# Second expert table: 768 of its 2048 columns read whole and multiplied, the other 1280 gathered

## The reference, cut to what matters

```python
sc = einsum('thcd,hckd->thck', qry, sub_keys)            # 256 tokens, 8 heads, 2 halves, 128 keys
top_s, top_i = top_k(sc, 16)
cand_s = top_s[:, :, 0, :, None] + top_s[:, :, 1, None, :]
cand_i = top_i[:, :, 0, :, None] * 128 + top_i[:, :, 1, None, :]
best_s, best_pos = top_k(cand_s, 16)
idx, gates = take_along_axis(cand_i, best_pos), softmax(best_s)
u   = expert_down[ib]                                    # 128 rows of 2048 for each token
act = gelu(einsum('tkd,td->tk', u, xb))
vv  = expert_up[ib]                                      # 128 rows of 2048 for each token
out = einsum('tk,tkd->td', gates * act, vv)
```

## Time and profile before

| | |
|---|---|
| median of three runs | 2442.86 us |
| the profiled execution, its time | 2440.96 us |
| its span, first to last instruction | 2439.2 us |
| busy: TensorE matmuls, VectorE, ScalarE, GpSimd | 2017.3, 1354.1, 623.8, 630.3 us |
| moved by DMA over the span | 727.64 MB, mean 298 GB/s |
| of it by the gathers | 536.90 MB |
| expert stage: first gather, last added row | 539.0 us, 1882.5 us |

### The profile page before, as it was taken

One profiled execution on the slowest core, in us unless ns is written; L12 is line 12 of the kernel. 1 busy time (PEld: TensorE's weight loads), 2 busy tenths in 40 slices (PEclk: granted clock), 3 DMA queues, 4 the chain that ended last, 5 costly groups with the idle time before them and its releaser, 6 DMA issues. The chain is left out here.

```text
span 2439.2 us, 21677 instructions
## 1 busy us (share of the span) xinstructions
PE 2017.3 (83%) x8013; PEld 1331.2 (55%) x8013; DVE 1354.1 (56%) x1820; ACT 623.8 (26%) x901; POOL 630.3 (26%) x523
## 2 busy tenths in 40 slices
PE   6999867984988989777777888898771899999975
PEld 5888746873444444322233434443220888999874
DVE  4446537447554556455555654665547755555444
ACT  4334325321011111111111111011001554354333
POOL 0000000006543544445355434444533000000000
PEclk9999958996999999999999999999996899999988
DMA  5555501729999999999999999999998544465531
GB/s 197 197 195 190 199 1 47 264 85 382 421 422 422 422 421 422 423 421 419 421 422 420 416 422 421 416 420 423 421 422 343 180 160 158 146 205 186 188 122 70
DMA packets 102203, 727.64 MB, mean 298 GB/s; under 512 B 11840, under 2 KB 11968, under 8 KB 19808
## 3 DMA queue, kind: packets, MB, share of 16 engines
q0 software_dynamic: 73728, 536.90, 53.1%
q1 hardware_dynamic: 28384, 189.52, 22.0%
HBM read 722.18 MB, written 4.19 MB: 298 GB/s over the span
## 5 line engine op out<-in xcount | busy, mean ns | idle before, releaser
L1248 PE MATMUL bank<-ring,work 128*128 128x512 f32 x1920 | 894.0, 609 | 240.1 <-DMA ring<-in_peer_up_dram,work 238.7
L1492 DVE CUSTOM_DVE_ANT_0 ring<-ring,mix_t 128x2048 f32<-128x2048 f32 x256 | 584.2, 2291 | 526.7 <-DMA ring<-in_peer_down_dram,work 526.5
L1248 PEld LDWEIGHTS bank<-ring,work 128*128 128x128 f32 x1920 | 350.5, 192 | 716.5 <-issue 504.3
L449 DVE TENSOR_TENSOR ring_r<-ring,ring_r 128x2048 fp32r<-128x2048 f32 (+2 forms) x150 | 320.0, 2136 | 319.4 <-ACT ring_r L428 319.0
L1376 POOL DMA_INDIRECT ring<-in_peer_down_dram,work x256 | 316.6, 1237 | 440.1 <-DVE work L1449 238.2
L1385 POOL DMA_INDIRECT ring<-in_peer_up_dram,work x240 | 284.4, 1185 | 480.4 <-PE bank L1248 421.6
L482 PE MATMUL bank<-ring_r,mix_r 128*128 128x512 f32 (+1 forms) x1248 | 393.2, 386 | 0.0
L428 ACT ACTIVATE ring_r<-ring 128x2048 fp32r<-128x2048 f32 (+2 forms) x150 | 267.6, 1787 | 307.1 <-DMA ring<-in_w_out_dram 90.4
L482 PE MATMUL bank<-ring_r,act_r 128*128 128x512 f32 (+1 forms) x864 | 309.4, 388 | 12.6 <-DVE ring_r L449 12.6
L1316 ACT ACTIVATE work<-const,work 128x128 f32<-128x128 f32 x240 | 91.5, 399 | 734.3 <-PE bank L1248 733.1
L482 PEld LDWEIGHTS bank<-ring_r,mix_r 128*128 128x128 f32 x1248 | 233.6, 188 | 43.5
(11 more groups left out here) (354 smaller groups left out, 1336.3 us busy)
## 6 DMA issues: line engine op xcount, KB each, us to landing
ring<-in_w_out_dram SPq DMA_DIRECT2D x32, 1024.0 KB, 4.8
ring<-in_w_in_qk_dram SPq DMA_DIRECT2D x24, 1024.0 KB, 4.8
ring<-in_w_in_rest_dram SPq DMA_DIRECT2D x24, 1024.0 KB, 4.8
ring<-in_w_in_mo_dram SPq DMA_DIRECT2D x24, 768.0 KB, 4.4
h<-in_w_query_dram SPq DMA_DIRECT2D x8, 2048.0 KB, 10.4
ring<-in_w_in_ml_oz_dram SPq DMA_DIRECT2D x12, 1024.0 KB, 4.8
h<-in_xa_wkv_dram SPq DMA_DIRECT2D x4, 2048.0 KB, 16.8
ring<-in_w_in_lru_dram SPq DMA_DIRECT2D x8, 1024.0 KB, 4.9
```

The costliest lines, as they stand in the source:

```text
L449: dve.tensor_tensor(low(c), raw(c), plain(high(c)), ALU.subtract).then_inc(k.weights_low, 1)
L1248: m = pe.matmul(B[c][:, :], diag[:, j % DEPTH, :], up_row(j)[:, c * 512:(c + 1) * 512], start=first, stop=last)
L1492: dve.tensor_tensor_reduce(down_row(j), down_row(j), xn[:, t, :], 1.0, 0.0, ALU.mult, ALU.add, dots[:, p, j:j + 1]).then_inc(down_used, 1)
```

## The change

The second table is stored as two: columns 0 to 767 (`peer_up_dense`, laid out as 128 blocks, one for each first key, of 128 second keys by 768) and columns 768 to 2047 (`peer_up_rest`).

- Of the 256 second-table gathers all remain, with 1280 columns (640 KB) instead of 2048. Five a unit ("near", 75 in units 1 to 15, of the unit before) are issued among the first-table gathers and added by TensorE, three matmuls each. The other 181 ("far") are issued after the last first-table gather, through four slots, and added by VectorE.
- For the 768 columns a matrix of coefficients is made for each tile: for each token q a product of two one-hot matrices of [row, key], one of them scaled by the coefficient, gives [second key, first key]. Four tokens make a group of one bank, which ScalarE copies into `w_t[t]`, 64 KB a partition. Tile 0's one-hots are made by ScalarE in units 8 to 14 (`first_hots`: 8 Abs, 1 Relu, 4 Copy for a group of four tokens); tile 1's by VectorE after the last unit, two instructions for each token.
- TensorE then multiplies all 128 blocks: SyncE loads a block of 384 KB (`dense`, four slots), and for each there are four products of 384 columns. VectorE adds the four banks at the end.
- The first table's gathers, their four slots, the selection and its place are as before. The four slots of the second table are now of 1280 columns, the rest of the half is for blocks and one-hots. Coefficients and expert numbers of all units are kept. `coef` of a unit is made at row 1 of the next.
- The memory's load comes at the stage's start; its transposes stand in unit 6 and its keys and values in units 6 to 8. The unit loops are written out instead of hardware loops.

```diff
 
 
+DENSE = 768
+REST = D - DENSE
+NEAR = 5
...
+    up_rows = shaped(k.ring[:, 0:DEPTH * REST], DEPTH, REST)
+    dense_rows = shaped(k.ring[:, DEPTH * REST:8192], DEPTH, DENSE)
+    down_rows = shaped(k.ring[:, 8192:16384], DEPTH, D)
+    HOTS = 2 * DENSE // (2 * P)
+    hots = shaped(k.ring[:, 8192 - 2 * DENSE:8192 - 2 * DENSE + HOTS * 2 * P], HOTS, 2, P)
+    w_t = [shaped(k.first_weights[:, :], P, P), shaped(k.second_weights[:, :], P, P)]
+    cuts = [(at, min(512, REST - at)) for at in range(0, REST, 512)]
+    half = DENSE // 2
...
+    near = lambda n: [(NEAR * (n - 1) + i, i) for i in range(NEAR)] if n else []
+    NEAR_ALL = NEAR * (UNITS - 1)
+    far_of = [[(n, j) for n in range(t * PEER_H, (t + 1) * PEER_H) for j in range(NEAR if n < UNITS - 1 else 0, K)] for t in range(NT)]
+    shorter = min(map(len, far_of))
+    far = [of[i] for i in range(shorter) for of in far_of] + [r for of in far_of for r in of[shorter:]]
+    landed = lambda u: (up_in[u % DEPTH], 16 * (u // DEPTH + 1))
+
+    first_groups = [(n, j) for n in range(PEER_H, UNITS - 1) for j in BUILD_AT if n > PEER_H or j > 9][:GROUPS]
+    assert len(first_groups) == GROUPS
+    memory_parts = {(6 + (8 + i) // K, (8 + i) % K): (i // 8, (2 * i % 16, 2 * i % 16 + 1)) for i in range(32)}
...
+            def dense(i):
+                sp.dma_start(dense_rows[:, i % DEPTH, :], ins["peer_up_dense"][i]).then_inc(dense_in[i % DEPTH], 16)
+
+            sp.wait_ge(mem_turned, TURNS)
+            sp.wait_ge(coef_done, UNITS - 1)
+            dense(0)
+            dense(1)
+            sp.wait_ge(hot_used, 2 * P)
+            dense(2)
+            dense(3)
+            for i in range(DEPTH, P):
...
+            def add_row(u, i, n):
+                t = (n - 1) // PEER_H
+                first, last = (n - 1) % PEER_H == 0 and i == 0, n in (PEER_H, UNITS - 1) and i == NEAR - 1
+                if first and t:
+                    pe.wait_ge(acc_out, len(cuts))
+                pe.wait_ge(diag_ready, u + 1)
+                pe.wait_ge(*landed(u))
+                for b, (at, width) in enumerate(cuts):
+                    m = pe.matmul(B[b][:, 0:width], diag[:, u % 2, :], up_rows[:, u % DEPTH, at:at + width], start=first, stop=last)
+                m.then_inc(up_used, 1)
...
+            def build_group(t, g, depth):
+                n = t * GROUPS + g
+                if n == 0:
+                    pe.wait_ge(query_out, KV1)
+                if n >= 3:
+                    pe.wait_ge(weights_out, n - 2)
+                for e in range(4):
+                    q = 4 * g + e
+                    pe.wait_ge(hot_ready, t * P + q + 1)
+                    pe.matmul(bank_of(n)[:, e * P:(e + 1) * P], hots[:, q % depth, 0, :], hots[:, q % depth, 1, :],
+                                  start=True, stop=True).then_inc(hot_used, 1)
...
+            turn_indices(1)
+            for g in range(GROUPS):
+                build_group(1, g, HOTS)
+            pe.wait_ge(weights_out, 2 * GROUPS)
+            pe.wait_ge(acc_out, NT * len(cuts))
+            for i in range(P):
+                pe.wait_ge(dense_in[i % DEPTH], 16 * (i // DEPTH + 1))
+                for t in range(NT):
+                    for c in range(2):
+                        m = pe.matmul(B[2 * t + c][:, 0:half], w_t[t][:, i, :], dense_rows[:, i % DEPTH, c * half:(c + 1) * half],
+                                      start=i == 0, stop=i == P - 1)
+                m.then_inc(dense_used, 1)
...
+            def take_group(t, g):
+                n = t * GROUPS + g
+                act.wait_ge(hot_used, 4 * n + 4)
+                act.activation(w_t[t][:, :, 4 * g:4 * g + 4], shaped(bank_of(n)[:, :], 4, P).rearrange("p t i -> p i t"), ACT.Copy) \
+                   .then_inc(weights_out, 1)
+
+            def first_hots(g):
+
+                if g == 0:
+                    act.wait_ge(iota_in, 16)
+                    act.wait_ge(indices_out, 1)
+                    act.wait_ge(mem_turned, TURNS)
+                else:
+                    act.wait_ge(hot_used, 4 * g)
+                for e in range(4):
+                    q = 4 * g + e
+                    act.activation(hots[:, e, 0, :], iota, ACT.Abs, bias=turned[:, 1, q:q + 1], scale=-1.0)
+                    m = act.activation(hots[:, e, 1, :], iota, ACT.Abs, bias=turned[:, 0, q:q + 1], scale=-1.0)
+                step(m)
+                all4 = hots[:, 0:4, :, :].rearrange("p a b c -> p (a b c)")
+                step(act.activation(all4, all4, ACT.Relu, bias=k.c("ones")[:, 0:1], scale=-1.0))
+                for e in range(4):
+                    act.activation(hots[:, e, 0, :], hots[:, e, 0, :], ACT.Copy, scale=turned[:, 2, 4 * g + e:4 * g + e + 1]) \
+                       .then_inc(hot_ready, 1)
...
+            for n in range(UNITS):
+                rows_here = dict(zip(NEAR_AT, near(n)))
+                pool.wait_ge(selected, n + 1)
                 for j in range(K):
+                    d = n * K + j
+                    if d >= DEPTH:
+                        pool.wait_ge(down_used, d - DEPTH + 1)
+                    gather(down_rows[:, d % DEPTH, :], ins["peer_down"], rows[:, n, j:j + 1], down_in[d % DEPTH])
+                    if j in rows_here:
+                        u, i = rows_here[j]
+                        if u == 0:
+                            pool.wait_ge(mem_squared, NT)
+                        if u >= DEPTH:
+                            pool.wait_ge(up_used, u - DEPTH + 1)
+                        gather(up_rows[:, u % DEPTH, :], ins["peer_up_rest"], rows[:, n - 1, i:i + 1], up_in[u % DEPTH])
+            for f, (n, j) in enumerate(far):
+                u = NEAR_ALL + f
+                if f < DEPTH:
+                    pool.wait_ge(up_used, u - DEPTH + 1)
+                else:
+                    pool.wait_ge(far_used, f - DEPTH + 1)
+                gather(up_rows[:, u % DEPTH, :], ins["peer_up_rest"], rows[:, n, j:j + 1], up_in[u % DEPTH])
...
+            select(0, 0)
+            for n in range(UNITS):
+                p, t = n % 2, n // PEER_H
                 for j in range(K):
+                    if j == 1 and n:
+                        weigh(n - 1, 1 - p)
+                    if j == 2 and n == PEER_H + 1:
+                        take_sums(0)
+                    if j == DEPTH and n + 1 < UNITS:
+                        select(n + 1, 1 - p)
...
+                    d = n * K + j
+                    row = down_rows[:, d % DEPTH, :]
+                    dve.wait_ge(down_in[d % DEPTH], 16 * (d // DEPTH + 1))
+                    dve.tensor_tensor_reduce(row, row, xn[:, t, :], 1.0, 0.0, ALU.mult, ALU.add, dots[:, p, j:j + 1]) \
+                       .then_inc(down_used, 1)
+            take_sums(1)
+            weigh(UNITS - 1, 1)
+
+            dve.wait_ge(indices_out, 2)
+            dve.wait_ge(hot_used, P)
+            for q in range(P):
+                if q >= HOTS:
+                    dve.wait_ge(hot_used, P + q - HOTS + 1)
+                dve.tensor_scalar(hots[:, q % HOTS, 0, :], iota, turned[:, 1, q:q + 1], turned[:, 2, q:q + 1], ALU.is_equal, ALU.mult)
+                dve.tensor_scalar(hots[:, q % HOTS, 1, :], iota, turned[:, 0, q:q + 1], None, ALU.is_equal).then_inc(hot_ready, 1)
...
+            dve.wait_ge(acc_out, NT * len(cuts))
+            last_of = {}
+            for f, (n, j) in enumerate(far):
+                t = n // PEER_H
+                if t in last_of:
+                    dve.wait_ge(far_used, last_of[t] + 1)
+                last_of[t] = f
+                u = NEAR_ALL + f
+                dve.wait_ge(*landed(u))
+                dst = k.x3[:, t, DENSE:D]
+                dve.scalar_tensor_tensor(dst, up_rows[:, u % DEPTH, :], coef[:, n, j:j + 1], dst, ALU.mult, ALU.add).then_inc(far_used, 1)
+            dve.wait_ge(dense_used, P)
+            for t in range(NT):
+                for c in range(2):
+                    dst = k.x3[:, t, c * half:(c + 1) * half]
+                    dve.tensor_tensor(dst, B[2 * t + c][:, 0:half], dst, ALU.add)
```

More of the change, by code:

```diff
@@ L1081, in peer @@
     hot = area.take(2, K, K)
+    diag = area.take(2, P)
+    area = Area(k.work[:, 4096:6144])
+    coef = area.take(UNITS, K)
+    rows = area.take(UNITS, K).bitcast(U32)
+    pairs = area.take(2, UNITS, K)
+    turned = area.take(3, P)
+    iota = area.take(P)
+    mem_ms, mem_sd, mem_rstd = area.take(NT), area.take(NT), area.take(NT)
     top = area.take(2, 2, K)
@@ L1254, in _ @@
-            walk(unit)(pe)
+            score(1, 1)
+            query(2, 0, range(KC))
+            score(2, 0)
+            pe.wait_ge(stored, 1)
+            for n in range(1, UNITS):
+                rows_here = dict(zip(NEAR_AT, near(n)))
+                for j in range(K):
+                    if n + 2 < PEER_H:
+                        query(n + 2, n % 2, [j])
+                    if n == 6 and j < TURNS:
+                        turn_memory(j)
+                    if (n, j) in memory_parts:
```

(67 more changed lines are left out.)

387 lines of the change are left out of this document (140 added, 247 removed).

## The result

The changed kernel takes 2594.38 us, the median of four runs (2593.33 to 2599.62), against 2442.24 for the kernel before, also of four: a ratio of 1.063, 95% interval 1.0612 to 1.0649. It is slower by 152 us, where +65 was forecast and the range ended at 2580. The sign was right, the size was not.

What follows compares the result with a forecast made beforehand. The prediction took the expert stage as bound by DMA bytes at 421 GB/s, with slots limiting during selections. Terms -119.5 + 98 + 25 + 50 + 17 - 5 gave +65 us: 2507 us from 2442, range 2435 to 2580.

Steps and rivals of the forecast that it cites:

- slots as the second limit: Expert stage: during a VectorE selection no first-table slot comes free, so slots limit DMA there, as seen in unit 0.
- Bytes: Second-table traffic: gathers save 100.7 MB, blocks bring back 50.3 MB; net 50.3 MB less, -119.5 us.
- The pause: Selections in units 1 to 14: DMA idle at least 6.6 us, taken as 7 each, +98 us in all.
- One-hots: After the last unit: VectorE's 256 one-hot instructions for tile 1, 52 us, within a +50 us term.
- ScalarE's one-hots: Tile 0's one-hots on ScalarE: 9.6 us a group, 48 us for five in a unit of 57, so hidden.
- Rival 1: Selection pauses: query loads fill them, 35 of the 98 us go, total 2421 us; chance 0.14.
- Rivals 3, 4 and 5: 3: half-clock TensorE tail, 2787 us (chance 0.04); 4: no change, 2443 to 2450 (0.05); 5: no bytes saved, 2627 (0.03).
- Issue of gathers: Near part, units 1 to 15: gather instructions lengthened beside VectorE thin the supply by 3%, +25 us (0 to 45).
- Far rows and blocks: Last part of the stage: far rows and blocks near full DMA take 410 us (ends 393 and 448), +17 us.
- two-stage picture: Last part: once blocks are done DMA is no longer full, a far row taking 2.1 us through four slots.
- Rival 2: All transfers: smaller ones run below 421 GB/s, total 2534 to 2576 us; chance 0.14.
- the shorter tail: Stage end after the last bytes: some 4 us instead of 9, -5 us (ends -6 and 0).

Runs made afterwards that it cites:

- run 3: Changed kernel with VectorE summing each first-table row (one input, one column written) instead of multiplying it with the token's row: 2535.95 us.
- Run 4: Changed kernel without the blocks' loads, products and last bank sums, far rows kept on four slots: 2553.09 us.
- run 5: Changed kernel without the blocks' loads, products and sums, and with six far-row slots instead of four: 2449.50 us.
- run 2: Changed kernel with each first-table dot product reading 1024 columns instead of 2048, every byte still moved: 2514.70 us.

## Why the prediction fell short

**What held.** DMA as the bound before, and slots as the second limit, read from unit 0. Bytes: -50 MB, as counted. The pause, nearly: forecast 7 us from a 6.6 us floor; without the blocked issue (run 3) it costs 8.1 in the mean of 14, 15 us more in all. One-hots: forecast 52 us, measured 1526.1 to 1584.0, 57.9, or 0.45 us for a token's two; with sums and turns 61.2 against 58. ScalarE's one-hots and the near rows' products stayed covered: VectorE waited 2.1 us in all for gelu. TensorE did not bound the end by its clock: 1.00 beside the blocks, 332 us for them against 345 worked out. Rival 1 (loads in the pauses) came for one load of the seven, at 1017 us, whose window moved 303 GB/s and the other thirteen 222 to 268; the other units with a load took some 5 us more, the load's own time. Rivals 3, 4 and 5 did not come.

**The first step that failed: "Issue of gathers", +25 us.** The near part was to end at about 1475 and ended at 1522.8, 48 us late. I had the mechanism, 0.93 and 2.24 us for one instruction, and sized its effect at 3%, from four rows of VectorE in unit 0 that lie 2.57 us apart instead of 2.49; the upper end was 45. Run 3 measures it as 57 us, 32 more than the term; with the 15 of the longer pauses that is 47 of the 48. Unit 0 of the kernel before already showed more than I read. GpSimd's gathers there, and DMA over the same time:

```profile
587.26 2.20 POOL L1376 DMA_INDIRECT ring<-in_peer_down_dram,work  x1 [0.30 <-issue]
...
589.77 2.46 POOL L1376 DMA_INDIRECT ring<-in_peer_down_dram,work  x1 [0.30 <-issue]
...
583.00:597.00 14.00, 0.00 (x0) 0.00 (x0) 12.01 (x12) 0.00 (x0) 11.49 (x5) 0.50 0.97 373
```

Each gather is held and the next follows at once, so GpSimd itself has become the slow one, and DMA moves 373 GB/s, 11% under 421. The four rows of VectorE did not show it in full. In the changed kernel it is the same: in 1086 to 1124 above, 17 gathers and the 0.30 us between them fill some 35 of 38 us. The near gathers stand in the same queue and add to it, but unit 0 has none, so they are not the cause by themselves.

The term also rests on a rule that I set against the row. The Trainium skill, SBUF — State Buffer, "Practical consequences", says that an instruction with two SBUF inputs contends with a GpSimd instruction that reads SBUF. I read it as leaving gathers out. The groups name `work` among a gather's sources, in the earlier trace rows and above: it reads its 128 row numbers from SBUF. Run 3 agrees with the rule so read, at 942 ns with one input and 1825 with two, and so does the sum with one input in PSUM, at 0.94 us. That the gather's read of its numbers is the access that is blocked was not tried by itself.

**The second, and the largest miss: "Far rows and blocks", taken at 410, measured 450.5** (1584.0 to 2034.5), 40 us more than the term. The step that failed is the choice of a value near full DMA. The two-stage picture in that part was right and I left it. Beside the blocks a far row took about 2.57 us. The sum had TensorE's 345 us covered by DMA; in fact TensorE worked nearly without a gap and waited 0.9 us for blocks, so its products set the 332 us (330 to 336 in every run that has them). DMA moved 397 GB/s in that time instead of 421, some 19 us over 332. Whether DMA or the four slots held the far rows there was not separated. After the blocks a row took 2.3 (2.1 was worked out), and some 51 rows were left: 117 us. Run 4 and run 5 show that rows without blocks beside them are bound by slots, not bytes. The upper end, 448, held it nearly; the choice of 410 did not.

**The third is the range.** All terms at their upper ends gave +167, which holds the 152 measured, but the range stopped at +137, since I let the ends of separate terms average out. They share one cause, too little in flight, and went the same way together.

Rival 2, that small transfers run below 421 GB/s, named the symptom and the wrong cause. The size was not what ruled here: six far gathers of 640 KB in flight moved 403 GB/s at VectorE's pace, four moved 292. The number in flight counted, at the same size. The Trainium skill, DMA: Bandwidth & Descriptors, "Bandwidth", wants 1 MiB in a transfer for 75% of peak; these runs do not show that loss where several are in flight: with the one-input sum (run 3), gathers of 1 MB and 640 KB in turn moved 421 GB/s between the windows.

Where the 120 us of saved bytes went, term by term against a stage at full DMA: -119.5; 14 pauses of 8.1 as in run 3, +113; the blocked issue by run 3, 22 of it in those pauses, +57; the one-hots between the parts, 61.2 less the 8 of data that was on its way, +53; the end, 450.5 against (168.9 - 3.4) MB at 421, which is 393, +57; the shorter tail, -5. That is +155.5, and the stage became 154 longer. Run 3 is one execution, so its two terms are sure to a few us.

## What to carry to other kernels

When a stage is bound by bytes, ask what keeps the queue full while its consumer does something else, before counting what fewer bytes save; take away one of two streams and the other must carry both the pauses and the latency. A gather's issue that overlapped the long two-input product here waited for its end: try to cut such an instruction in two or four, look in the trace whether gathers then get in between, and put the transfers with free slots directly in front of the pause. The blocked issue that cost 4 us in the kernel before, with eight slots, cost 57 with four. And read a stage's supply from its DMA rate over all that lies between two pauses, not from a few rows of its consumer.

## What the runs showed of the hardware

- An indirect gather's instruction on GpSimd took 0.94 us beside a one-input reduction of 2048 columns. With the two-input product of the same length in its place the mean of all 256 was 1.83; 1.26 and 1.09 when the product was cut in two and four.
- A gather that was held ended 0.8 us after the VectorE instruction, both for the two-input product and for a TENSOR_SCALAR of 2048 columns in place with one tensor from SBUF. Beside a sum with one input from PSUM and 512 columns written to SBUF it was not held (0.94 us). Under back-to-back far rows one waited to the end of all of them, 4.42 us, and one in run 5 6.81 us; others got in between two.
- Far rows of 5 KB a partition and blocks of 3 KB together moved 397 GB/s at a DMA share of 1.01; rows of 8 KB alone moved 421. In run 5 rows of 5 KB alone moved 403 at a share of 1.00, in step with VectorE, and the near part 387 at 0.98 where the same sizes moved 415 at 1.00 in run 2. So a share near 1 does not by itself show that no more could be moved.
- TensorE's granted clock was 0.50, its lower level of 1.2 GHz, at 1082 to 1084 us, where TensorE waits in a pause, and 0.66 in the 38 us from 1086, where it works a little over half the time; through the 58 us of one-hot products it was 0.95, and beside the blocks 1.00, the level of 2.4 GHz. At the lower levels TensorE had time to spare (busy 0 of 2 us and 21 of 38), and through the one-hots VectorE was busy for all of the 57.9 us.
